# A gated-delta recurrence rearranged: products without the state ahead for all chunks, and centred values

## The reference, cut to what matters

```python
def step(S, inp):
    r_t, w_t, k_t, v_t, kk_t, a_t = inp
    sa = einsum('bhvk,bhk->bhv', S, -kk_t)
    S = S * w_t[:, :, None, :] + sa[..., None] * (kk_t * a_t)[:, :, None, :] + v_t[..., None] * k_t[:, :, None, :]
    return S, einsum('bhvk,bhk->bhv', S, r_t)
y = rwkv7_scan(r, decay, k, v, kk, a)
mean = jnp.mean(y, axis=-1, keepdims=True)
var = jnp.mean(jnp.square(y - mean), axis=-1, keepdims=True)
y = (y - mean) * lax.rsqrt(var + RWKV_GN_EPS) * ln_w.reshape(H, N) + ln_b.reshape(H, N)
y = y + jnp.sum(r * k * r_k, axis=-1, keepdims=True) * v
```

## Time and profile before

| | us |
|---|---|
| median of 3 runs | 2165.74 |
| profiled execution, its own time | 2172.61 |
| its span | 2171.4 |
| PE busy / PEld busy | 2030.9 / 1613.2 |
| DVE busy / ACT busy | 1088.7 / 873.4 |

### The profile page before, as it was taken

How to read it: one execution, slowest core, us unless ns; L and a number is a source line. 1 busy time by engine, 2 the same in 40 slices (tenths; PEclk the granted TensorE clock), 3 DMA queues, 4 the chain that set the end, 5 groups by cost and what they waited for, 6 DMA issues and landing times.

```text
span 2171.4 us, 28244 instructions
## 1 busy us (share of the span) xinstructions
PE 2030.9 (94%) x11400; PEld 1613.2 (74%) x11400; DVE 1088.7 (50%) x1929; ACT 873.4 (40%) x1567; POOL 27.3 (1%) x68
## 2 busy tenths in 40 slices
PE   6898888889989999999999999999899999999997
PEld 5765666777766679878888887667478978888886
DVE  5666468737465454354334354444355445343444
ACT  5325443244345444343223243566644344232332
POOL 0000000000000000000000000011000000000000
PEclk9989899999999999999999999999999999999999
DMA  5210011012211123122222222111023212222221
GB/s 200 88 49 21 20 59 49 3 60 101 88 49 49 39 97 127 68 88 97 90 104 89 98 95 88 59 49 49 30 97 113 102 59 97 97 97 97 97 97 69
DMA packets 52050, 169.63 MB, mean 78 GB/s; under 512 B 5776, under 2 KB 9424, under 8 KB 51920
## 3 DMA queue, kind: packets, MB, share of 16 engines
q1 hardware_dynamic: 51920, 167.82, 22.1%
HBM read 165.70 MB, written 2.10 MB: 77 GB/s over the span
## 4 chain that ended last, share of the span: by engine, by line
PE 85%; DVE 9%; ACT 4%; issue 1%; DMA 0%; POOL 0%; SPq 0%; DVEq 0%; ACTq 0%
PE ps L152 83%; PE ps L157 3%; DVE ps L380 1%; DVE wr L171 1%; DVE X L1530 0%; DVE lo L218 0%; DMA cst<-d_cst 0%; DVE macc L233 0%; DVE ra_S L769 0%; DVE rc_S L769 0%; DVE rb_S L769 0%; DVE ra_Z L789 0%; ACT sa_sp L2103 0%; DVE x_acc L233 0%; ACT wr L165 0%
## 5 line engine op out<-in xcount | busy, mean ns | idle before, releaser
L152 PE MATMUL ps<-hi,wr 128*128 128x512 f32 (+1 forms) x4616 | 1406.9, 385 | 50.1 <-DVE wr L171 34.2
L152 PEld LDWEIGHTS ps<-hi,wr 128*128 128x128 f32 x4616 | 861.9, 190 | 230.2 <-DVE wr L171 25.7
L152 PE MATMUL ps<-lo,wr 128*128 128x512 f32 (+1 forms) x2308 | 879.9, 381 | 0.0
L152 PEld LDWEIGHTS ps<-lo,wr 128*128 128x128 f32 x2308 | 439.6, 190 | 84.1 <-issue 3.9
L165 ACT ACTIVATE wr<-raw 128x1024 fp32r<-128x1024 f32 x293 | 307.6, 1052 | 349.6 <-PE ps L152 349.6
L171 DVE TENSOR_TENSOR wr<-raw,wr 128x1024 fp32r<-128x1024 f32 x293 | 356.7, 1217 | 4.3 <-ACT wr L165 2.3
L1457 DVE TENSOR_TENSOR X<-X,ps 128x512 f32<-128x512 f32 x96 | 66.0, 688 | 238.3 <-PE ps L152 238.3
L1986 ACT ACTIVATE mlp<-mlp 128x512 f32<-128x512 f32 x64 | 40.4, 632 | 207.8 <-DVE mlp L1969 207.8
L1969 DVE SCALAR_TENSOR_TENSOR mlp<-ps,R 128x512 f32<-128x512 f32 x64 | 44.3, 692 | 113.2 <-PE ps L152 106.2
L213 ACT ACTIVATE hi<-X,pv 128x512 fp32r<-128x512 f32 x48 | 34.7, 722 | 138.2 <-DVE X L1457 136.2
L1972 DVE TENSOR_TENSOR lo<-mlp,hi 128x512 fp32r<-128x512 f32 x64 | 44.3, 693 | 87.8 <-ACT hi L1990 87.8
(11 more groups left out here) (696 smaller groups left out, 1877.4 us busy)
## 6 DMA issues: line engine op xcount, KB each, us to landing
raw<-d_w SPq DMA_DIRECT2D x128, 512.0 KB, 3.4
raw<-d_wkv SPq DMA_DIRECT2D x32, 512.0 KB, 3.5
raw<-d_w_in SPq DMA_DIRECT2D x30, 512.0 KB, 3.5
raw<-d_sb_w_in SPq DMA_DIRECT2D x24, 512.0 KB, 3.4
raw<-d_ev_w_in SPq DMA_DIRECT2D x16, 512.0 KB, 3.4
raw<-d_wq SPq DMA_DIRECT2D x16, 512.0 KB, 3.5
raw<-d_wo SPq DMA_DIRECT2D x16, 512.0 KB, 3.4
X<-d_xT SPq DMA_DIRECT2D x16, 256.0 KB, 5.1
```

The lines of the kernel that those rows point to most:

```text
L152: return pe.matmul(out, lhsT, rhs, start=start, stop=stop, skip_group_check=True)
```

## The change

For each pair the 12 steps of the rounds and the step of the mean become fewer, and a pair has 28 steps. `L.center` is the identity less a 64th of the block of ones; v is turned by a product with it. Step 9 also turns `kk` (`kx`), step 11 (level 1) computes `u` for all chunks from `S4` and `vt`; ScalarE puts both beside each other into `KB`. Step 22 gives `XF` times `[kx, u]` for all chunks (`ab`: the parts A, B). In step 23 follow the first state, `pt` (A turned times `bt`, with the identity added: what carries a state on) and `g` (A times `S4`, added to `r`'s rows). Steps 24 to 26 hold the states 1 and 2 and two double outputs, step 27 the `var` product. The state `M` holds 64 columns per chunk.

```diff
@@ inverse_tensor (step 9, and step 11 where l == 1)
+    b = K.take(*k, "kx")
+    for c in range(4):
+        done = tr(pe, M, b[:, c * 128:c * 128 + 128], L.KR(c, 0))
...
+        if l == 1:
+            b = K.take(*k, "u")
+            for c in range(4):
+                for h in range(2):
+                    at = c * 128 + h * 64
+                    done = mm(pe, b[:, at:at + 64], L.S4[c][h][:, 0:128], L.vt[:, at:at + 64], at == 0, True)
@@ inverse_scalar calls it for kx in step 9 and for u in step 11
+def columns_scalar(K, a, k, L, name):
+    a.wait_ge(*K.done("pe", *k, name))
+    for z in range(2):
+        to = L.KB[z].rearrange("p (j w q) -> p j w q", j=4, w=2)[:, :, 0 if name == "kx" else 1, :]
+        a.activation(to, r3(K.bank(*k, name)[:, z * 256:z * 256 + 256], 4), ACT.Copy).then_inc(
@@ rwkv_tensor
+            if name == "vt":
+                done = mm(pe, r3(b[:, cs], 2), src[:, cs], sh.center, c == 0, True)
+            else:
+                done = tr(pe, M, b[:, cs], src[:, cs])
...
-    for c in range(4):
-        ... (12 steps: u, xu, y and m of each chunk)
-    mm(pe, b, M.C("blk"), M.Y[i], True, True).then_inc(*K.tell("pe", *k, "mean"))
-    yield
+    pe.wait_ge(*K.done("act", *k, "u"))
+    pe.wait_ge(*K.done("dve", *k, "XF"))
+    for z in range(2):
+        b = K.take(*k, "ab", z)
+        for j in range(4):
+            at = z * 512 + j * 128
+            done = mm(pe, b[:, j * 128:j * 128 + 128], L.XF[:, at:at + 128], L.KB[z][:, j * 128:j * 128 + 128],
+                      j == 0, True)
+    yield
+    pe.wait_ge(*K.done("act", *k, "ab", 0))
+    state_tensor(K, pe, k, L, 0)
+    pe.wait_ge(*K.done("dve", *k, "ab", 1))
+    for c in (1, 2):
+        for h in range(2):
+            done = mm(pe, b[half(h), c * 64 - 64:c * 64], L.A(c, h), L.bt[:, c * 128 + h * 64:c * 128 + h * 64 + 64],
+                      c == 1, True)
+    for c in (1, 2, 3):
+        for h in range(2):
+            done = mm(pe, b[half(h), c * 128 - 128:c * 128], L.A(c, h), L.S4[c][h][:, 384:512], c == 1, True)
+    yield
+    state_tensor(K, pe, k, L, 1)
+    outputs_tensor(K, pe, k, L, 0)
+    yield
+    state_tensor(K, pe, k, L, 2)
+    yield
+    outputs_tensor(K, pe, k, L, 1)
+    yield
...
+def state_tensor(K, pe, k, L, c):
+    for h in range(2):
+        at = slice(c * 128 + h * 64, c * 128 + h * 64 + 64)
+        mm(pe, b[half(h), 0:64], L.kt[:, at], L.vt[:, at], True, False)
+        done = mm(pe, b[half(h), 0:64], L.bt[:, at], L.B(c, h), False, not c)
+    if c:
+        for h in range(2):
+            done = mm(pe, b[half(h), 0:64], L.PT[half(h), c * 64 - 64:c * 64], L.M[half(h), c * 64 - 64:c * 64],
+                      False, True)
+def outputs_tensor(K, pe, k, L, z):
+    for c in (2 * z, 2 * z + 1):
+        out = [b[half(h), c % 2 * 128:c % 2 * 128 + 128] for h in range(2)]
+        for h in range(2):
+            mm(pe, out[h], L.vt[:, c * 128 + h * 64:c * 128 + h * 64 + 64], L.S4[c][h][:, 128:256], c % 2 == 0, False)
+        for h in range(2):
+            done = mm(pe, out[h], L.B(c, h), L.S4[c][h][:, 384:512], False, not c)
+        if c:
+            for h in range(2):
+                done = mm(pe, out[h], L.M[half(h), c * 64 - 64:c * 64], L.KR(c, 1)[half(h), :], False, True)
@@ rwkv_vector
-        ... (L1009, L1012, L1017; L1023, the mean)
+    v.tensor_copy(L.AB[1], K.bank(*k, "ab", 1)) ...
+    v.tensor_tensor(r3(L.PT, 2), r3(K.bank(*k, "pt")[:, 0:128], 2), wide(sh.eye, 2), ALU.add) ...
+    v.tensor_tensor(L.KR(1, 1), L.KR(1, 1), b[:, 0:128], ALU.add) ...
+    v.tensor_tensor(r, r, r3(b[:, 128:384], 2), ALU.add) ...
+def state_vector(K, v, k, L, c):
+    v.tensor_scalar(L.M[:, c * 64:c * 64 + 64], K.bank(*k, "m", c)[:, 0:64], L.st[:, 4 + c:5 + c], None, ALU.mult)
@@ rwkv_scalar
-        ... (12 copies of 128x128: u, xu, y of each chunk; the square of y less its mean)
+    a.activation(L.AB[0], K.bank(*k, "ab", 0), ACT.Copy) ...
+def outputs_scalar(K, M, a, k, i, L, z):
+    b, to = K.bank(*k, "y", z)[:, 0:256], slice(z * 256, z * 256 + 256)
+    a.activation(L.tmp2[:, to], b, ACT.Square).then_inc(*K.tell("act", *k, "y", z))
+    a.activation(M.Y[i][:, to], b, ACT.Copy) ...
```

## The result

The kernel after takes 2180.61 us (median of 6 runs, 2177.75 to 2181.83) against 2169.09 for the kernel before (6 runs on the same chip): ratio 1.005, 95% interval 1.0038 to 1.0063. That is 11.5 us more, where +4 was forecast. The forecast of 2170 stood on a kernel before at 2165.7 us; on that scale the measured difference gives 2177.2. The profiled execution took 2181.33 us.

A forecast was written before the change was run, and what follows sets the result against it. The prediction took the kernel to be bound by what PE issues. Stages summed to +2.5 us, and passes +6, waits +2, half clock -3 to +5; it took +4 on 2165.7, so 2170 us, range 2146 to 2190.

The forecast's parts named there:

- five stages: A to E, from A0's rounds to the first `w_out` product; forecast 32.5, 82, 72, 60 and 28 us.
- likeliest case: The forecast of 2170 us, counted with rounds that were already covered; own range 2160 to 2178, chance 0.46.
- slower by more: Outcome above 2176.6 us, beyond the 0.5% (10.8 us) that measurement can tell from no change; chance 0.29.
- stage B: NSA steps 29 to 40, to stand beside A1's steps 1 to 12; 82 us for 54.4, waits 18 for 7.5.
- stage E: Last rounds and tail, to the first `w_out` product; 28 us instead of 42, as A1's rounds move to earlier stages.
- Who stands beside whom: A1 starts at step 29 instead of 37, so NSA's scaling queues behind A1's VectorE lists; 18 us of waits in B.
- Rival 1: The denses hide NSA's chain: waits of B stay 7.5, C's fall to 4; -9.5, or 2156 us; chance 0.25.
- Rival 2: VectorE becomes the bound in B and D: B loses 27 us, passes at the high end; 2187 us; chance 0.29.
- Passes, +6: PE passes of the new products less those gone: +1.5 us per pair, +6 for four pairs (-2 to +14).
- Waits, +2: PE's waits over the stages from A0's rounds to `w_out`: 42 us for 40.
- Half clock, -3: Time PE loses at half clock: 3 us less, as the scores' thin products no longer run alone.
- Steps before A, +2: A0's steps ahead of stage A: +0.65 and +0.5, and `u` at 1.8, part falling into waits; +2 us.

The follow-up runs named there:

- e1: Kernel after with eight idle steps between A0 and A1, so A1 starts at step 37 as before; 2169.92 us, 1.0013 to the kernel before.
- e5: Kernel after with VectorE's order alone changed in steps 28 to 37: second NSA pair's scaling ahead of the recurrence's list, maxima behind; 2177.1 us, 1.0036.
- e7: Kernel after with `u` of each pair issued four steps later, in step 19 for step 11; 2178.77 us, 1.0039 to the kernel before.
- e10: Kernel after with eight idle steps spread between A0's last eight steps and `u` four steps later; 2166.63 us, 0.9984 to the kernel before.
- e4: Kernel before with v centred by a product, without the mean product and its subtraction, all 36 steps kept; 2168.11 us, 0.9996.
- e6: Kernel before, old products, with A0's round steps merged so that A0 has 28 steps and A1 starts eight earlier; 2193.35 us, 1.0108.
- e3: Kernel after with the two lanes exchanged on every engine, NSA's instructions ahead of those of A0 and A1; 2175.37 us, 1.0042.
- e2: Kernel after with twelve idle steps between A0 and A1, so A1 goes in step with B and C; 2176.82 us, 1.0043.
- e9: Kernel after with eight idle steps, one behind each of A0's last eight steps; 2171.2 us, 1.0014 to the kernel before.

## Why the prediction was right, and where its sizes were not

The forecast was +4, to 2170, from the same five stages; the measured difference is +11.5, at the edge of the 0.5% (the interval is 0.38 to 0.63%). 2180.6 lies inside the whole range, 2146 to 2190, but that range was wide. It is above the likeliest case's own range (2160 to 2178), and even at 2177.2, on the scale of the forecast, it falls among "slower by more", to which I gave 0.29. The mechanism was the forecast one; the size was not, and the sum came as near as it did because errors of both signs met: stage B was 4 us longer and stage E 5 us shorter than forecast, and the passes cost 8 us less, the waits 4 us more. Part of the hit is luck.

- **Who stands beside whom.** Right. The waits for the scaling behind A1's list came in the steps forecast: 6.62 for 5.5 in step 4, 2.25 for 3 in step 3, 20 us in stage B for 18. That the scaling waits come from the pairing is shown by e1 (2.0 us of them left), and that they come from the place in VectorE's queue by e5 (none left). What they cost is less than their sum: e5 gains 3.5 us and e1 9 to 11. Rival 1 is out; its mark was under 10 us of waits. The slow stretch that I looked for behind these waits came once: the clock was 0.51 from 289 to 295 us, behind the wait of 6.62, and 1.00 from 275 to 281, behind that of 2.25.
- **Rival 2, VectorE the bound.** Its mark was a loss of 27 us in stage B, which lost 20. But e5 gives it something: once the scaling was early, the maxima were late, and the ratio came out in the range of the expectation that VectorE's work, and not its order, holds PE.
- **Passes, +6.** The mis-sized term. PE's timeline of B and C in the last rounds:

```profile
474.17 2.05 PE L152 MATMUL ps<-rb_KB,rb_XF 128*128 128x128 f32 x16
476.05 1.95 PE L152 MATMUL ps<-rc_KB,rc_XF 128*128 128x128 f32 x16
477.93 0.34 PE L152 MATMUL ps<-rb_vt,rb_kt 128*64 128x64 f32 x4
478.21 0.41 PE L152 MATMUL ps<-rb_bt,rb_AB 128*64 128x64 f32 x8
478.45 0.83 PE L152 MATMUL ps<-rb_S,rb_AB 128*64 128x128 f32 x12
479.11 0.34 PE L152 MATMUL ps<-rc_vt,rc_kt 128*64 128x64 f32 x4
```

  By the distance of starts `ab` is 1.88 (forecast 2.35), the eight passes of the first state 0.28, or 0.035 each (forecast 0.07 to 0.11), `pt` 0.24 (0.5) and `g` 0.66 (0.9); three states with what `PT` adds come to 1.6 for 2.5, and v's turning to 0.89, the low end. With the 1.95 that go, a pair costs about 0.5 less than before instead of 1.5 more: -2 for four pairs in place of +6, just under my low ends taken together (-0.4 a pair). I had priced passes with 64 weight columns from rows of 16 in one place (0.067 each) and from groups of four with 128 moving columns (0.27, so 0.07 each), while the states have 64 moving columns and alternate between the heads' halves. The Trainium skill's page "TensorEngine Tiling (Array Packing)", Key Properties, says that different tiles work in parallel; the 0.035 agrees with it, and I had leaned to the dear end. PE's busy time is 3.6 us up and not 2 down, since passes at half clock stay busy for longer (`u` 3.67 for 2.00): it is 5.1 us less in the five stages, and 5.9 more from 119 us to A, with `kx`, v and A0's `u` there at a clock of 0.87 for 0.90.
- **Waits, +2.** All stages together have 46 us for 40: +6. Against the forecast of each stage B has 20 for 18, C 9.1 for 7, D 7.2 for 10, and E its 5.75 ahead of `w_out`. C's two long weight waits came out at 3.25 and 2.25 for 4 and 2.
- **Half clock, -3.** Length times what the granted clock lacks to 1, which counts idle time too, falls from 17.3 to 12.4 us in the five stages by an estimate from the two tables of windows, and rises by 3.6 from 119 us to A (0.90 of 97.9 us, 0.87 of 103.1). That rise is part of the next point.
- **Steps before A, +2.** The other term that was mis-sized: +5.3 in the profiled pair, +5.5 from 119 us to A in the mean of two traces each. I priced `kx` and v (1.15) and let `u` fall into waits. It fell into a stretch at 0.50 of the clock, at 3.67 us, and full clock came back later (0.68 from 169 to 179 us, against 0.94 in the first trace of before). The stretch itself was at 0.50 in that trace of before as well. E7 and e10 show that moving `u` brings the NSA dense forward; how much of the 5.3 is `u` and how much the spread of the clock between runs they don't separate.
- **Stage E, 28.** 22.95: the cheaper passes (2 us in the first states with `pt` and `g`, 0.7 in `ab`) and none of the 2 us of single waits. B was 4 us longer instead (86.2 for 82), so the sum of the five stages still came out right because two errors met.
- **Behind `w_out`, 0.** +2.1, in both traces of each kernel, where no instruction was changed. The same part takes 1678.3 us in e4 and 1682.9 in e6, both with the old products, and 1680.9 (e3) to 1683.8 (e2) with the new ones, so the difference may be spread. It stays open.

## What to carry to other kernels

Where two lanes are interleaved step by step by hand, removing steps from one is a change of everything behind it. Price the new neighbours first, above all a short operation of one lane that another engine awaits and that now stands behind a long list in an in-order queue; and try the shorter lane padded back to its old length, which restores the old pairing. Here that took back three quarters of the loss (e1) and was no gain over the kernel before; with `u` later as well it was 2.0 us faster (e10). Work pulled forward can land in a stretch at half clock: `u` cost 3.67 us there and 2.00 where the clock was up. But look at the whole time too, since e7 lost most of that gain again further on.

## What the runs showed of the chip that I had not expected

- Two traces of the same kernel differ by 5.6 us at the first `w_out` product (490.94 and 485.38), and the differences sit where the granted clock does: 0.81 and 0.90 over the first 50 us or so behind the dense at 119 us, 0.57 and 1.00 in the twelve microseconds that begin 24 us behind the NSA dense.
- Float32 passes with 64 weight columns cost 0.035 us with 64 moving columns and 0.055 with 128 when they alternate between the halves, against 0.117 for 128 by 128 (`ab`, 16 in 1.88).
- A gain of 6.5 us ahead of the NSA dense (e7) was taken back to 1.2 behind it, where nothing but `u` of the other pairs had moved (against the second trace of the kernel after, 5.5 and 0.1); in the old pairing (e10 against e9) the late `u` gained 2.7 ahead of that dense and 3.2 behind it (107.31 and 262.21 became 104.64 and 259.01, in one trace each, 5.9 us where the medians say 4.6).
